# Rows of the experts' results leave through ScalarE's DMA queue instead of GpSimd's

## The chip, the cores and the metric
One core of a Trainium2 chip. The time is the device time of one execution in microseconds, the median over runs. A core has TensorE (PE), VectorE (DVE), ScalarE (ACT), GpSimd (POOL) and SyncE (SP), and 16 DMA engines that serve the queues of all of them. SP's and ScalarE's transfers go through hardware queues, GpSimd's through a software queue.

## The reference
A decoder trunk of two layers over 1024 tokens of width 1024, in float32. Each layer is: a mixer (attention in layer 0; a state-space layer and gated DeltaNet in layer 1), a mixture of 32 experts of which each token takes two, and a gated embedding:

```
h = h + mixer(rms_norm(h))
h = h + hier_moe(rms_norm(h))      # per expert: (silu(x @ w_gate) * (x @ w_up)) @ w_down, 1024 -> 512 -> 1024
h = h + sigmoid(rms_norm(h) @ w_g + b_g) * (p @ w_p)
```

The change touches the experts' stage alone. Its weights are 32 x 3 matrices of 2 MB in a layer, about 201 MB.

## The kernel before, in words
**The experts' block.** Before it, GpSimd scatters each token's row to a region of its expert in DRAM (`slots_in`). `first_blocks` (from L1615) then works through units of 128 rows. A unit is a whole expert (the first two), or parts of two experts: 64 + 64 or 96 + 32 rows. There are 21 units in a layer (`units`, from `expert_units`, L1065). `weight_order` (L1094) fixes in which order the 2 MB tiles of w_gate, w_up and w_down are loaded, and into which of eight places of a ring each goes. SP issues these loads (L1669), each after the product that used the place's last tile.

**The engines in one unit n.** TensorE: the first half of the gate product of unit n, the transposes of the hidden rows of unit n-1 (L1736), the second half of the gate product, the two halves of the down product of n-1, the transposes of the rows of n+1 (`turn`, L1716), the up product of n. All products stand on L1724. ScalarE: Silu of the gate (L1788), a copy of the first half of the results of unit n-1 (`y_half`, L1781), a copy of the transposed rows of n+1 (`turned_out`, L1775). VectorE: a copy of the transposed hidden rows (L1801), the second half of the results (L1807), gate times up (L1840). GpSimd: `rows_in(n + 2)` brings the rows of unit n+2 from `slots_in` once the rows of unit n are transposed (L1689), and `rows_out(n - 1)` takes the results of unit n-1, once ScalarE and VectorE have both copied their half, to `slots_out` in DRAM (L1695). A part of a unit is one transfer. The expert's number is known when the kernel is built for the first two; for the others it is loaded from a table on the chip into a register of the issuing engine.

**What orders the work around it.** There are two buffers for the rows and two for the results, taken by even and odd units. `y_half` on both engines waits for the results of two units earlier to have left (`y_out`). The last unit's results don't go through `rows_out`: SP issues them (`last_rows`, L1679). SP does this after the embedding's own loads (L1948 to L1958), which are in the same block of the program and wait for places of the ring to come free. Then SP waits for all results to be in DRAM and gives `all_out` (L1564). The embedding's part (`layer_embedding`, from L1962) has GpSimd gather two rows of `slots_out` for each token (L2010), VectorE add them to h (L2172, L2175), and the gate product follow on TensorE (L2080).

**Overflow.** `overflow_blocks` handles rows beyond an expert's share; with these inputs its loop runs over nothing.

Of the kernel before, what the change touches and what calls it, by code (L numbers as in the profile page):

```python
# [15 lines left out]
P = 128  # L16
# [1032 lines left out]
EXPERTS = GROUPS * PER_GROUP  # L1049
REGION = S + P // 2  # L1050
ROUTES = GROUPS + EXPERTS
HEAVY, FIXED, FIRST = 18, 2, 1e5
# [12 lines left out]
def expert_units():  # L1065

    heavies, lights = list(range(FIXED, HEAVY)), list(range(HEAVY, EXPERTS))
    ranks, units = list(range(FIXED)), [[Part(q, 0, P)] for q in range(FIXED)]  # L1070
    trios, pairs = len(heavies) // 2, (len(lights) - len(heavies) // 2) // 2
    assert 2 * trios == len(heavies) and trios + 2 * pairs == len(lights)

    def pair():
        q = len(ranks)
        ranks.extend([lights.pop(0), lights.pop(0)])
        units.append([Part(q, 0, 2 * QUAD), Part(q + 1, 2 * QUAD, 2 * QUAD)])

    for n in range(pairs - 1):
        pair()  # L1080
    for n in range(trios):
        q = len(ranks)
        ranks += [heavies.pop(0), heavies.pop(0), lights.pop(0)]
        units += [[Part(q, 0, 3 * QUAD), Part(q + 2, 3 * QUAD, QUAD)],
                  [Part(q + 1, 0, 3 * QUAD), Part(q + 2, 3 * QUAD, QUAD, QUAD)]]
    pair()
    return ranks, units
# [527 lines left out]
def first_blocks(nc, c, t, layer, r, ch, ring, preloaded, place, joint):  # L1615
# [6 lines left out]
    views = expert_weights(t, layer)  # L1622
    KF = FF // P
    _, units = expert_units()
    UNITS = len(units)
    tiles, places, last_user = weight_order(units)
    at_tile = {tile: n for n, tile in enumerate(tiles)}
    arrivals = [sum(len(units[m]) for m in range(n % 2, n + 1, 2)) for n in range(UNITS)]
    with scope(joint) as ctx:
        xb, y = place[:, 0:2], place[:, 2:4]  # L1630
# [8 lines left out]
        with stage(nc, *[f"tile{n}_in" for n in range(RING)], "x_turned", "x_copied", "gated", "silued", "upped", "hidden", "h_turned",  # L1639
# [3 lines left out]
            x_in, y_out = c.x_in, c.y_out  # L1643
# [14 lines left out]
            @block.sync  # L1658
            def _(sp):
                expert = {}  # L1660
                for n in range(preloaded, len(tiles)):
                    kind, q = tiles[n]
                    if q not in expert:
                        expert[q] = q if q < FIXED else sp.value_load(r.table[0:1, 3, q:q + 1], min_val=0, max_val=EXPERTS - 1)
                    before = [x for x in range(n) if places[x] == places[n]]
                    if before:
                        used, by = tiles[before[-1]][0], last_user[tiles[before[-1]]]
                        sp.wait_ge((gated, upped, downed)[used], (2 if used == 2 else 1) * (by + 1))
                    sp.dma_start(ring[places[n]].rearrange("p (k n) -> p k n", k=KF if kind == 2 else KD),  # L1669
                                 views[kind][expert[q]]).then_inc(tile_in[places[n]], 16)  # L1670
                clear_used(sp)
                last_expert.update(expert)
# [8 lines left out]
            @block.gpsimd  # L1681
            def _(pool):
                expert = {q: q for q in range(FIXED)}

                def rows_in(n):
                    for x in units[n]:
                        if x.q not in expert:
                            expert[x.q] = pool.value_load(r.table[0:1, 3, x.q:x.q + 1], min_val=0, max_val=EXPERTS - 1)
                        pool.dma_start(xb[x.row:x.row + x.rows, n % 2], c.slots_in[bass.ds(expert[x.q] * REGION + x.slot, x.rows), :]).then_inc(x_in[n % 2], 16)  # L1689

                def rows_out(n):
                    pool.wait_ge(y_act, n + 1)
                    pool.wait_ge(y_dve, n + 1)
                    for x in units[n]:
                        pool.dma_start(c.slots_out[bass.ds(expert[x.q] * P + x.slot, x.rows), :], y[x.row:x.row + x.rows, n % 2]).then_inc(y_out[n % 2], 16)  # L1695

                for n in range(UNITS):
                    if n + 2 < UNITS:
                        pool.wait_ge(x_turned, n + 1)
                        rows_in(n + 2)  # L1700
                    if n:
                        rows_out(n - 1)
                for n in (UNITS - 3, UNITS - 2):
                    pool.wait_ge(y_out[n % 2], y_before[n % 2] + 16 * arrivals[n])

# [63 lines left out]
            @block.scalar  # L1769
            def _(act):  # L1770
                def turned_out(n):
                    act.wait_ge(x_turned, n + 1)
                    if n >= 2:
                        act.wait_ge(upped, n - 1)
                    act.activation(xbt[:, n % 2].rearrange("p k t -> p (k t)"), turned[:], ACT.Copy).then_inc(x_copied, 1)  # L1775

                def y_half(n):
                    act.wait_ge(downed, 2 * n + 1)
                    if n >= 2:
                        act.wait_ge(y_out[n % 2], y_before[n % 2] + 16 * arrivals[n - 2])  # L1780
                    act.activation(y[:, n % 2, 0:SLAB], py[:, 0:SLAB], ACT.Copy).then_inc(y_act, 1)  # L1781

                turned_out(0)
                for n in range(UNITS):
                    act.wait_ge(gated, n + 1)
                    if n:
                        act.wait_ge(hidden, n)
                    act.activation(gate, pg[:], ACT.Silu).then_inc(silued, 1)  # L1788
                    if n:
                        y_half(n - 1)  # L1790
                    if n + 1 < UNITS:
                        turned_out(n + 1)
                y_half(UNITS - 1)

            @block.vector
# [1629 lines left out]
```

## Time and profile before

| | us |
|---|---|
| median of 3 runs | 3043.67 |
| lowest, highest | 3043.55, 3053.84 |
| the profiled execution's own time | 3048.08 |
| its span | 3046.6 |
| TensorE busy, ScalarE busy, GpSimd busy | 2795.1, 662.1, 249.7 |

The span is from the first to the last instruction in the trace; the execution's own time is taken around it. The experts' stages lie at about 830 to 1400 us and 2340 to 2920 us. "Busy" does not count the issuing of a transfer by SP or ScalarE; rows of such issues carry the name of the queue (SPq, ACTq). GpSimd's issues are counted as busy.

### The profile page before, as it was taken

What the parts mean: (1) busy time and instruction counts of PE and PEld (TensorE: products, weight loads), DVE (VectorE), ACT (ScalarE), POOL (GpSimd) and SP (SyncE); (2) the same over time, 40 slices, a digit from 0 to 9 for tenths busy, and PEclk for the clock granted to TensorE, in tenths of its full rate; (3) what the DMA queues carried; (4) which work ended last, traced back from release to release, by engine and by line L of the source; (5) the groups of instructions that cost most, each with busy time, mean ns of one, the idle gap of its engine ahead of it and who ended that gap; (6) DMA issues with size and microseconds to landing.
All of it is one profiled execution on the core that took longest, in us unless ns stands there. A gap on an engine that the chain in (4) does not pass through costs nothing. (4 is left out here: it accounts for less than half of the span.)

```text
span 3046.6 us, 40782 instructions
## 1 busy us (share of the span) xinstructions
PE 2795.1 (92%) x16517; PEld 1438.2 (47%) x16518; DVE 1113.5 (37%) x2450; ACT 662.1 (22%) x1262; POOL 249.7 (8%) x376
## 2 busy tenths in 40 slices
PE   7999999999898898989989999877998989888998
PEld 4644555555642232324467744477655323222343
DVE  2585455544400000004464725566464000000053
ACT  3310355541110000003421124422211000000132
POOL 0000000000100000002000000044211000000020
PEclk9999999999899999999999999998998999999999
DMA  4000693012599999996020120000417999999931
GB/s 162 28 20 8 243 408 123 1 65 99 218 353 397 397 397 397 401 410 218 35 67 1 16 71 28 0 2 2 175 63 271 368 399 397 399 400 393 400 127 42
DMA packets 137045, 609.37 MB, mean 200 GB/s; under 512 B 25700, under 2 KB 32260, under 8 KB 120456
## 3 DMA queue, kind: packets, MB, share of 16 engines
q1 hardware_dynamic: 111848, 529.08, 44.7%
q0 software_dynamic: 21632, 74.46, 6.9%
q10 hardware_dynamic: 3376, 3.19, 0.3%
q8 instruction: 133, 2.18, 0.3%
q14 instruction: 56, 0.46, 0.0%
HBM read 503.80 MB, written 101.71 MB: 199 GB/s over the span
## 5 line engine op out<-in xcount | busy, mean ns | idle before, releaser
L2775 PE MATMUL acc<-xt,work 128*128 128x512 f32 x384 | 166.9, 593 | 0.0
L672 PE MATMUL acc<-h,xt 128*128 128x512 f32 x384 | 165.2, 592 | 0.0
L310 PE MATMUL scores<-xt 65*128 65x512 f32 (+7 forms) x384 | 146.0, 489 | 0.4 <-DVE xt L451 0.4
L1724 PE MATMUL pg<-place 128*32 128x512 f32 (+2 forms) x736 | 137.8, 594 | 2.5 <-issue 2.5
L457 DVE TENSOR_REDUCE nmax<-scores 128x1 f32<-128x256 f32 (+7 forms) x128 | 96.8, 756 | 74.0 <-PE scores L312 70.4
L672 PEld LDWEIGHTS acc<-h,xt 128*128 128x128 f32 x384 | 72.9, 190 | 91.1 <-issue 90.9
L1724 PE MATMUL pu<-place 128*32 128x512 f32 (+2 forms) x768 | 115.1, 639 | 0.5 <-issue 0.5
L1221 PE MATMUL acc<-place 128*128 128x512 f32 x256 | 112.7, 594 | 1.1 <-PEq L71 1.1
L2775 PEld LDWEIGHTS acc<-xt,work 128*128 128x128 f32 x384 | 72.0, 190 | 86.1 <-issue 86.1
L1807 DVE COPY place<-py 128x512 f32<-128x512 f32 x21 | 14.5, 692 | 230.0 <-PE py L1724 230.0
L1807 DVE COPY work<-py 128x512 f32<-128x512 f32 x21 | 14.5, 691 | 228.9 <-PE py L1724 228.9
L404 ACT ACTIVATE s_t<-scores,nmax 128x256 f32<-128x256 f32 (+7 forms) x128 | 94.3, 736 | 8.0 <-DVE nmax L457 6.6
L1724 PE MATMUL py<-place 128*32 128x512 f32 (+2 forms) x608 | 86.5, 606 | 9.1 <-issue 7.9
L768 ACT ACTIVATE place<-acc 128x256 f32<-128x256 f32 (+4 forms) x88 | 39.8, 473 | 243.1 <-PE acc L672 243.0
L1840 DVE TENSOR_TENSOR work<-work,pu 128x512 f32<-128x512 f32 x21 | 14.4, 688 | 201.6 <-PE pu L1724 201.6
L1840 DVE TENSOR_TENSOR place<-place,pu 128x512 f32<-128x512 f32 x21 | 14.4, 688 | 200.0 <-PE pu L1724 200.0
L2449 PE MATMUL acc<-s_t,xt 128*128 128x260 f32 (+1 forms) x256 | 85.5, 496 | 1.1 <-PEq L71 1.1
L310 PEld LDWEIGHTS scores<-xt 65*128 65x128 f32 (+1 forms) x384 | 62.8, 190 | 33.1 <-issue 32.7
L1788 ACT ACTIVATE place<-pg 128x512 f32<-128x512 f32 x21 | 12.5, 597 | 293.4 <-PE pg L1724 293.4
L1724 PE MATMUL pg<-xt,place 128*32 128x512 f32 (+2 forms) x400 | 75.0, 601 | 1.3 <-ACT place L1775 1.1
L672 PE MATMUL acc<-place,xt 128*128 128x392 f32 (+1 forms) x256 | 76.1, 453 | 0.0
L1724 PE MATMUL pg<-own,work 128*32 128x512 f32 (+2 forms) x400 | 74.8, 601 | 1.4 <-ACT work L1775 1.1
(761 smaller groups left out, 5435.5 us busy)
## 6 DMA issues: line engine op xcount, KB each, us to landing
place<-in_moe_w_gate_dram SPq DMA_DIRECT2D x21, 2048.0 KB, 24.2
place<-in_moe_w_up_dram SPq DMA_DIRECT2D x20, 2048.0 KB, 26.3
slots_out<-zeros SPq DMA_DIRECT2D x4, 9216.0 KB, 63.0
place<-in_moe_w_down_dram SPq DMA_DIRECT2D x18, 2048.0 KB, 27.1
xt<-in_moe_w_up_dram SPq DMA_DIRECT2D x17, 2048.0 KB, 26.4
xt<-in_moe_w_gate_dram SPq DMA_DIRECT2D x16, 2048.0 KB, 23.6
xt<-in_moe_w_down_dram SPq DMA_DIRECT2D x15, 2048.0 KB, 29.1
s_t<-in_moe_w_up_dram SPq DMA_DIRECT2D x11, 2048.0 KB, 26.8
```

The costliest lines, as they stand in the source:

```text
L310: pe.matmul(bank(n, u)[:, a * SLAB:a * SLAB + w], qkt[0:kind(p).rows, p % 2, u, 0, i * P:(i + 1) * P], qkt[0:kind(p).rows, p % 2, u, 1, a ...
L404: act.activation(probs[:, u, n % 2, 0:(i + 1) * P], bank(n, u), ACT.Exp, bias=nmax[:, n % 2, u:u + 1], accum_out=total[:, (n // NT) % 2, i ...
L457: dve.tensor_reduce(nmax[:, n % 2, u:u + 1], bank(n, u), AX.X, ALU.max, negate=True).then_inc(maxed, 1)
L672: last = pe.matmul(acc[:, n % 4, 0:width], xs[:, k, tile_of(i)], weights[:, k, cols], start=(k == 0), stop=(k == k_of - 1))
L768: last = act.activation(place, part, ACT.Copy)
L1221: last = pe.matmul(acc[:, n, :], columns(k, i), slabs[n][:, k, :], start=(k == 0), stop=(k == KD - 1))
L1724: last = pe.matmul(out[part], lhs[:, k, part], weights_of(kind, q)[:, k, cols], start=(k == 0), stop=(k == k_last), skip_group_check=True)
L1788: act.activation(gate, pg[:], ACT.Silu).then_inc(silued, 1)
L1807: dve.tensor_copy(y[:, n % 2, SLAB:D], py[:, SLAB:D]).then_inc(y_dve, 1)
L1840: dve.tensor_tensor(hid, gate, pu[:], ALU.mult).then_inc(hidden, 1)
L2449: ins = pe.matmul(acc[:, n % 4, 0:width], xt[:, k, at], slab[:, k, 0:width], start=(k == 0), stop=(k == KD - 1))
L2775: last = pe.matmul(acc[:, n % 4, :], slabs[m // 4 % 2][:, k, (m % 4) * P:(m % 4 + 1) * P], xt[:, k, half * SLAB:(half + 1) * SLAB], start= ...
```

## The change
`rows_out` moves from GpSimd's program to ScalarE's. GpSimd keeps `rows_in` alone. ScalarE issues the transfers of unit n-1 after the copy of the transposed rows of unit n+1, waits for both halves of the results first, and loads the experts' numbers into its own registers. The last unit's results stay with SP.

```diff
-                def rows_out(n):
-                    pool.wait_ge(y_act, n + 1)
-                    pool.wait_ge(y_dve, n + 1)
-                    for x in units[n]:
-                        pool.dma_start(c.slots_out[bass.ds(expert[x.q] * P + x.slot, x.rows), :], y[x.row:x.row + x.rows, n % 2]).then_inc(y_out[n % 2], 16)
-
-                for n in range(UNITS):
-                    if n + 2 < UNITS:
-                        pool.wait_ge(x_turned, n + 1)
-                        rows_in(n + 2)
-                    if n:
-                        rows_out(n - 1)
+                for n in range(UNITS - 2):
+                    pool.wait_ge(x_turned, n + 1)
+                    rows_in(n + 2)
                 for n in (UNITS - 3, UNITS - 2):
                     pool.wait_ge(y_out[n % 2], y_before[n % 2] + 16 * arrivals[n])
...
+                expert = {q: q for q in range(FIXED)}
+
+                def rows_out(n):
+                    act.wait_ge(y_act, n + 1)
+                    act.wait_ge(y_dve, n + 1)
+                    for x in units[n]:
+                        if x.q not in expert:
+                            expert[x.q] = act.value_load(r.table[0:1, 3, x.q:x.q + 1], min_val=0, max_val=EXPERTS - 1)
+                        act.dma_start(c.slots_out[bass.ds(expert[x.q] * P + x.slot, x.rows), :], y[x.row:x.row + x.rows, n % 2]).then_inc(y_out[n % 2], 16)
+
                 turned_out(0)
                 for n in range(UNITS):
...
                     if n + 1 < UNITS:
                         turned_out(n + 1)
+                    if n:
+                        rows_out(n - 1)
                 y_half(UNITS - 1)
```

## Rows read from the trace of the kernel before

**Rows 1.** The page: busy us, share of the span and instructions of each engine.
```profile
PE 2795.1 (92%) x16517; PEld 1438.2 (47%) x16518; DVE 1113.5 (37%) x2450; ACT 662.1 (22%) x1262; POOL 249.7 (8%) x376
```

**Rows 2.** Windows: us, busy PE, PEld, DVE, ACT, POOL (instructions), TensorE clock, DMA share, GB/s.
```profile
820.00:1400.00 580.00, 524.36 (x3808) 187.09 (x3807) 55.81 (x111) 55.99 (x80) 47.92 (x86) 0.96 1.00 387
...
2440.00:2820.00 380.00, 335.79 (x2878) 110.88 (x2878) 29.68 (x43) 31.61 (x43) 29.12 (x58) 0.96 1.02 398
```

**Rows 3.** Waits of TensorE from 2440 to 2820 us: total, times, longest.
```profile
PE turned L1716 <- issue: 24.4, 8, 3.9
PE py L1724 <- issue: 13.4, 7, 3.4
PE py L1724 <- DMA own<-in_moe_w_down_dram: 2.7, 3, 1.3
```

**Rows 4.** Chain of waits (start, us) and SP's issues, 2560 to 2610 us.
```profile
2567.57 26.14 DMA own<-in_moe_w_down_dram
...
2600.83 2.77 issue
...
2568.05 8.60 SPq L1669 DMA_DIRECT2D xt<-in_moe_w_up_dram  x2
```

**Rows 5.** Chain of waits, end of the second layer's experts: start, us, what.
```profile
2865.76 5.26 SPq L1952
...
2871.07 7.64 SPq L1954
...
2885.74 10.97 DMA slots_out<-work
```

**Rows 6.** Groups of ScalarE, 820 to 1400 us: busy, mean ns, idle before, releaser.
```profile
L1788 ACT ACTIVATE place<-pg 128x512 f32<-128x512 f32 x21 | 12.5, 597 | 293.4 <-PE pg L1724 293.4
```

**Rows 7.** Instructions of L1695: ns min/median/max; last its time to landing.
```profile
L1695 POOL DMA_DIRECT2D slots_out<-work x38: 489/510/583, 2373.5 to 2867.8; - x38
DMA to landing us min/median/max: 5.7/7.0/10.8
```

**Rows 8.** Timeline of GpSimd, 2470 to 2476 us; landing of its rows in (L1689).
```profile
2472.32 1.13 POOL L1695 DMA_DIRECT2D slots_out<-work  x2 [22.92 <-DVE work L1807]
2474.17 0.51 POOL L1689 DMA_DIRECT2D work<-slots_in  x1 [0.72 <-issue]
2475.37 0.49 POOL L1689 DMA_DIRECT2D work<-slots_in  x1 [0.69 <-issue]
...
DMA to landing us min/median/max: 7.6/9.0/17.3
```

**Rows 9.** SP's issues of the last rows: instructions of L1679, and the timeline.
```profile
L1679 SPq DMA_DIRECT2D slots_out<-place x2: 479/537/595, 1379.2 to 1380.0; - x2
...
2884.95 1.29 SPq L1679 DMA_DIRECT2D slots_out<-work  x2
```

**Rows 10.** Timeline of VectorE, 2860 to 2900 us.
```profile
2865.77 0.69 DVE L1807 COPY work<-py 128x512 f32<-128x512 f32 x1 [9.93 <-PE py L1724]
```

**Rows 11.** Timeline of ScalarE: one unit, and the last copy of y.
```profile
2499.36 1.02 ACT L1775 ACTIVATE work<-turned 128x1024 f32<-128x1024 f32 x1 [7.87 <-PE turned L1716]
2515.59 0.60 ACT L1788 ACTIVATE work<-pg 128x512 f32<-128x512 f32 x1 [15.20 <-PE pg L1724]
...
2879.67 0.60 ACT L1781 ACTIVATE work<-py 128x512 f32<-128x512 f32 x1 [16.74 <-PE py L1724]
```

**Rows 12.** DMA queues, 2440 to 2820 us: packets, MB, share of 16 engines.
```profile
q1 hardware_dynamic: 17513, 135.93, 89.6%
q0 software_dynamic: 4507, 14.79, 11.6%
```

**Rows 13.** DMA queues, 2867 to 2876 us.
```profile
q0 software_dynamic: 160, 0.52, 14.5%
```

**Rows 14.** SP's issues of weights (L1669), the group with the longest: ns min/median/max.
```profile
L1669 SPq DMA_DIRECT2D xt<-in_moe_w_up_dram x16: 332/453/6542, 844.8 to 2789.7; - x16
```

**Rows 15.** Timeline of VectorE, end of the first layer's experts.
```profile
1378.23 0.69 DVE L1807 COPY place<-py 128x512 f32<-128x512 f32 x1 [10.76 <-PE py L1724]
```

## Prediction

> **What bounds the kernel now.** The page first [rows 1]: TensorE is busy for 92% of the span and ScalarE for 22%, so a change of who issues a transfer can only matter where TensorE stops. The windows by stage say where that is [rows 2]: between 2440 and 2820 us, in the second layer's experts, TensorE is busy for 335.79 of 380 us, and the DMA column stands at 1.02 of the 16 DMA engines' time. Those engines have no free time there. The waits of TensorE in that stretch [rows 3] name a w_down tile for 2.7 us and "issue" for 37.8 us (24.4 + 13.4). I read most of that "issue" as weights too. In the chain of one pair of units [rows 4] the down products end at 2600.83 and TensorE starts on the turn of the next unit 2.77 us later. What stands between them in the code is the wait for the w_up tile. SP issued two w_up tiles in a run from 2568.05 to 2576.65, and I give them 26 to 27 us to land (26.14 is what the w_down tile before them took). The second one then lands near 2603, an estimate from these rows. So the loop is: a product ends and frees a tile place, SP issues the next 2 MB, and it lands 25 to 27 us later because others are under way: 2.1 MB at 398 GB/s is 5.3 us, so about five share the DMA engines. The bound is bytes over the DMA rate, with TensorE a close second, and the first layer is the same again.
>
> At the end of the block another chain takes over [rows 5]: SP issues the last unit's rows behind its issues of the embedding's weights, and the second transfer lands 10.97 us after 2885.74, at 2896.71; GpSimd's gathers wait for that.
>
> **The change, part by part.** The moved transfers are those of all units but the last. There are 21 units in a layer [rows 6], and the group on L1695 counts 38 transfers a layer, 76 in all [rows 7].
>
> 1. GpSimd loses 38 issues a layer, at 510 ns in the median [rows 7]. Its issues of rows for unit n+2 come up to 1.2 us earlier (two issues back to back took 1.13 us, at 2472.32 [rows 8]). These rows are wanted by TensorE's turn of unit n+2, more than one whole unit later (21 units in 580 us: 27 us each [rows 2]) and land in 9 us in the median [rows 8]. So they are not late now, and an earlier issue is worth 0.
>
> 2. ScalarE gains, in each unit, two waits, two issues and up to two loads of an expert number. SP issues the very same form of transfer for the last unit: 479 to 595 ns for the issue itself, 1.29 us for a pair with the register work between them [rows 9]. A load of the expert number is not shown on ScalarE. The nearest rows are GpSimd's: without loads a pair takes 1.13 us, so about 0.56 each; with a load between, the next issue starts 1.20 us after the one before (2474.17 to 2475.37) [rows 8]. That is about 0.65 us a load. Together 1.3 + 2 x 0.65 = 2.6 us a unit. Below, the bound is 0.5 us (issues overlapped with what ScalarE runs); above, I add two holds by SP (below). 28 loads a layer come in place of GpSimd's.
>
> They stand right after the turned copy (L1775). The y_act they wait for is ScalarE's own, done one operation earlier. The y_dve comes 0.69 us after the second down product [rows 10]; the turned copy, which itself takes 1.02 us [rows 11], can only begin after eight transposes that follow that product, so this wait costs nothing. Queued behind are the Silu of the next unit, which waits 293.4 us over 21 for TensorE's gate product, 14.0 us each [rows 6]. In the timeline: copy at 2499.36, done at 2500.38, next Silu at 2515.59, so 15 us of room [rows 11]. 2.6 of 14 us: price 0.
>
> 3. The DMA engines' work. The bytes are the same, and so is the number of row packets. What may differ is what a byte costs on the software and on the hardware queue. Over 2440 to 2820 us [rows 12] the hardware queue moved 135.93 MB in 89.6% of 380 x 16 engine-us, 24.95 GB/s an engine; the software queue 14.79 MB in 11.6%, 20.97 GB/s. But that queue carries rows in and rows out mixed. Between 2867 and 2876 us only rows out were on it [rows 13]: 0.52 MB in 14.5% of 9 x 16 = 144 engine-us, 25 GB/s. So the expensive ones are the rows in, which stay where they are. Rows out already cost what the weights cost. I take 0. The two bounds: with 20 units of 0.524 MB, 10.49 MB a layer, the mixed rate gives 500 engine-us against 420 on the hardware queue, 80/16 = 5 us saved a layer, 10 us in all; the other way, if such a write cost a tenth more on ScalarE's queue, 2.6 us a layer lost, 5 in all.
>
> 4. SP. While ScalarE issues, SP may have to wait. In the loop this delays a weight transfer's start by some 0.5 us while about five others are under way, and DMA stands at 1.02: nothing. At the end of the block it does not stand under that cover. The rows of the last unit but one are ready at 2866.46 (DVE's copy from 2865.77, 0.69 us [rows 10]), and SP issues nearly without a break from 2865.76 until it takes up the last rows at 2884.95 [rows 5, 9]. Two issues of 0.54 us in between would move SP's last rows by up to 1.1 us in this layer. But SP's issues are long there (7.64 us at L1954) against 0.33 us for a 2 MB tile where it is not held (the shortest of L1669 [rows 14]), so they wait for room in the queue, and that room comes at the same time whoever else issues. In layer 0 the last rows are issued at 1379.2 [rows 9], right after DVE's copy, which ends at 1378.92 [rows 15]; the copy is what they wait for, and a delay of SP is hidden there in part. I take 0.5 us for both layers together, with 0 and 2.2 as ends.
>
> The sum is 0 + 0 + 0 + 0.5. On the profiled execution's own time, 3048.08 us (the span 3046.6 and 1.5 around it), that is 3048.6. The profiled execution is 4.4 us above the median of the runs shown (3043.67), so in those terms 3044.2; I say 3044.
>
> A rule weighed against this. The trace shows SP in one issue for as long as 6542 ns in the loop [rows 14], and 7.64 us at the end [rows 5]; ScalarE issues no transfer in those stretches, so no row shows what it would do then. The Trainium skill (Perfetto Trace Analysis, DMA Instruction — HWDGE) states that the hardware descriptor generator is shared by the sequencers that use it and locked for one at a time, with the lock wait inside the profiled time. By that rule ScalarE would stand behind SP in such a stretch; by the rows alone it would not. Where it changes the time, it is the second rival.
>
> **Rivals.**
> Rows out get cheaper on the hardware queue. For it: the software queue's share per MB, 19% above the other one's in the mixed window. Against it: the window with rows out alone. Worked out above: 10 us less, 3034. If something else of the software path goes with it, such as GpSimd's issues of rows being late for TensorE, it would be more: the waits "issue" at TensorE's turn, 24.4 us in 380, are the only room, and if half of them were really rows in that come late, both layers would give 24 us, 3020. Against that: these rows land in 9 us and have 20. The Trainium skill (SBUF — State Buffer, the "DVE blocks DMA" trap) has software descriptors starved while VectorE copies; here GpSimd issues rows out only after VectorE's copy has ended and takes 489 to 583 ns each time, so no row shows a starved one.
>
> Slower, by one mechanism: the hardware queues of SP and ScalarE exclude each other while one issues. Place one is ScalarE, held in rows_out. It decides once it is held for more than about 11 us after the turned copy (14.0 less 2.6), because the Silu is then late and with it TensorE's next up product and gate. One hold in the loop is at most 6.5 us, so that needs two in a row. Place two is the block's end: if SP always goes first, ScalarE gets free only near 2884.9 instead of issuing at 2866.5, its last copy of y, at 2879.67 now [rows 11], comes 5 to 6 us late, and SP's last rows, which wait for it, go out near 2886.7 (two issues, 1.3, and the copy, 0.6, later): 1.8 us; in both layers about 3: 3047. Place three is SP, held by 76 issues of 0.54 us. If none of that were covered, 41 us, 3085; but for this the DMA engines would have to run dry, and nothing in rows 2 says so. A middle case, with ten or so late Silus or tiles of 2 us, is 3064.
>
> The change does not do what it says. Rows out landed in 7.0 us (5.7 to 10.8) before [rows 7]. Nobody waits for them inside the loop, because y of unit n is written again two units later. So a faster or slower landing changes nothing either way, and the time stays at 3044.
>
> **How the numbers follow.** Forecast, with the last rival, which gives the same time: 0.78. Cheaper rows by up to 10 us: 0.07. GpSimd's rows were late, 3020 or so: 0.04. Exclusion with a small price at the ends (3047): 0.06; with late Silus or tiles (3064 and up): 0.05. What a measurement of this kernel tells from no change is 0.5%, 15.2 us. Faster by more: 0.04, and 0.01 for what I don't see, 0.05. Slower by more: 0.05 and 0.02 for the same, 0.07. Within: 0.88. Range 3032 to 3058: the low end is the full 10 us and a little of the runs' own spread (3043.55 to 3053.84), the high end that spread with the price at the block's ends.
>
> **What would show it.** The page after: GpSimd's issues on the old line gone and 76 issues on ScalarE's queue; the small hardware queue q10 up by some 21 MB and the software queue down by as much. TensorE busy as before, DMA at 1.0 from 2440 to 2820, and the mean of GB/s within 1% of 398. ScalarE's issues near 0.54 us where SP is not in an issue; several us where it is, if the two exclude each other. The Silu still ended by TensorE's gate product. The chain at the end through SP's issues and the last rows as before. Wrong would be: a Silu released by anything but TensorE, TensorE idle for weights while the DMA share is under 1, or a stretch of the experts that is shorter by 5 us or more a layer.

## The result, and the profile after

The changed kernel takes 3022.18 us (median of 4 runs, 3019.68 to 3028.07), the kernel before 3044.39 beside it (4 runs). The ratio is 0.9917, with a 95% interval of 0.99 to 0.9933: 22 to 25 us less, where no change was forecast. A second measurement, the run change_again, gave 0.9916 (0.9899 to 0.9932).

The page of the changed kernel answers to [rows 1] like this:

```profile
PE 2797.8 (92%) x16517; PEld 1445.1 (48%) x16518; DVE 1114.0 (37%) x2450; ACT 662.6 (22%) x1262; POOL 210.9 (7%) x300
```

Only GpSimd has less to do than before. What has changed stands in the windows, which answer to the second row of [rows 2]:

```profile
2440.00:2820.00 380.00, 350.19 (x3024) 114.90 (x3020) 30.38 (x44) 32.22 (x44) 13.73 (x28) 0.96 1.02 411
```

The DMA engines are as full as before (1.02), but they move 411 GB/s, not 398, and TensorE gets through 3024 products in the window instead of 2878. The queues from 2440 to 2780 us (packets, MB, share of 16 engines), first before, then after:

```profile
q1 hardware_dynamic: 15969, 121.22, 89.3%
q0 software_dynamic: 4160, 13.63, 11.9%
```
```profile
q1 hardware_dynamic: 16357, 124.53, 89.7%
q0 software_dynamic: 2180, 7.17, 5.8%
q10 hardware_dynamic: 2225, 7.32, 5.7%
```

Read as MB over engine time (share x 340 x 16 us): before, the weights on q1 went at 24.95 GB/s an engine and the rows on q0 at 21.1. After, the weights go at 25.5, the rows in on q0 at 22.7 and the rows out on q10 at 23.6. So the gain is not mainly on the moved transfers. The weights, which nobody touched, have become cheaper.

A short window shows where. From 2499.4 to 2509.4 us before, and from 2492.5 to 2499.5 us after, the rows out and the rows in of one unit both move (1.04 MB of rows in each window):

```profile
DMA packets 912, 3.63 MB, mean 363 GB/s; under 512 B 89, under 2 KB 89, under 8 KB 891
```
```profile
DMA packets 723, 2.66 MB, mean 380 GB/s; under 512 B 77, under 2 KB 77, under 8 KB 722
```

Against 420 GB/s (the mean of the stage in the run wide_in below), 10 us at 363 lose 1.4 us and 7 us at 380 lose 0.7. That is 0.7 us a unit, and with 38 such units some 26 us, an estimate from these two windows.

ScalarE's new issues, the instructions of its line (ns min/median/max), and how long they took to land:

```profile
L1782 ACTq DMA_DIRECT2D slots_out<-work x38: 321/322/537, 2366.3 to 2847.7; - x38
...
DMA to landing us min/median/max: 6.0/7.7/11.8
```

They are shorter than the 0.54 us that I took, and none is held: the longest, in the first layer, has 563 ns. At 2847.19 ScalarE issues a pair in 0.81 us in the middle of SP's issue of 4.77 us (L1955, at 2845.74 in the chain below):

```profile
2847.19 0.81 ACTq L1782 DMA_DIRECT2D slots_out<-work  x2
```

The timelines of ScalarE and GpSimd in one unit of the changed kernel show where they stand:

```profile
2464.27 1.43 ACTq L1782 DMA_DIRECT2D slots_out<-work  x2
```
```profile
2464.71 0.51 POOL L1689 DMA_DIRECT2D work<-slots_in  x1 [23.60 <-issue]
2465.86 0.49 POOL L1689 DMA_DIRECT2D work<-slots_in  x1 [0.64 <-issue]
```

Rows out and rows in are now issued within half a microsecond of each other, on two queues. Before, they stood in one queue, out first, in 1.9 us later [rows 8], or 4.7 to 5.2 us later in the units between (2495.78 and 2501.01 in the next one). So the change did two things: it gave the rows out a queue of their own, and, as ScalarE issues them behind its turned copy, it moved them next to the rows in.

Where in the kernel: GpSimd's first gather after the experts starts at 1375.28 instead of 1389.97 in the first layer, and 1.5 us of these 14.7 were there before the block (the first copy of transposed rows starts at 832.45, not 833.95). That leaves 13.2 us. In the second layer the last scatter before the block starts at 2320.12 instead of 2326.35, the first gather at 2876.88 instead of 2897.08: 14.0 us. The sum is 27, or 28.6 with the 1.5; the spans differ by 20.2 (3046.6 and 3026.4). The rest is lost in between. From the first gather to the last scatter before the second block, which is mostly the second layer's mixer, it takes 936.4 us before and 944.8 after. The granted clock of TensorE differs there. From 1600 to 1800 us, before, after, and in the run called mirror below:

```profile
1600.00:1800.00 200.00, 190.68 (x919) 134.07 (x918) 100.51 (x252) 34.84 (x59) 7.34 (x21) 0.98 0.14 33
```
```profile
1600.00:1800.00 200.00, 191.29 (x887) 131.42 (x887) 93.25 (x188) 34.49 (x57) 7.35 (x21) 0.94 0.14 33
```
```profile
1600.00:1800.00 200.00, 190.95 (x909) 128.50 (x909) 95.59 (x203) 35.11 (x58) 7.35 (x21) 1.00 0.14 33
```

The clock there is 0.94 after and 1.00 in mirror, whose profiled execution took 3021.44 us against 3028.07. The same stage takes 943.0 us in change_again, a second profile of the changed kernel, 933.2 in mirror, 943.1 in apart and in two_wide, and 935.6 in over_read. Two_wide has its rows out on GpSimd and over_read on ScalarE, so the stage's length does not go by the engine that issues them. What sets it stays open; it puts up to 12 us into the times below that do not come from the experts' stages.

The chain at the end of the second layer's block is the same as in [rows 5], 20 us earlier: SP's issues of the embedding's weights, the last rows landing in 10.37 us, the gathers.

```profile
2845.74 4.77 SPq L1955
...
2850.55 8.68 SPq L1957
...
2859.27 4.64 SPq L1959
...
2863.96 1.11 SPq L1961
...
2866.14 10.37 DMA slots_out<-work
```

### The profile page after: what moved, and what is told of

It is laid out like the page before. It is cut to its first block and busy times, and to the rows that moved or that the text cites. A ratio compares the mean times of both kernels' runs of the same rounds, so it can differ in the third digit from the quotient of the medians.

```text
span 3026.4 us, 40948 instructions
## 1 busy us (share of the span) xinstructions
PE 2797.8 (92%) x16517; PEld 1445.1 (48%) x16518; DVE 1114.0 (37%) x2450; ACT 662.6 (22%) x1262; POOL 210.9 (7%) x300
## 5 line engine op out<-in xcount | busy, mean ns | idle before, releaser
L1789 ACT ACTIVATE work<-pg 128x512 f32<-128x512 f32 x21 | 12.5, 597 | 296.4 <-PE pg L1715 296.4
## 6 DMA issues: line engine op xcount, KB each, us to landing
xt<-in_moe_w_up_dram SPq DMA_DIRECT2D x17, 2048.0 KB, 25.5
```

## The experiments

"Ratio" is to the kernel before on the same chip, with the 95% interval. In all of them the DMA share from 2440 to 2780 us is 1.02 (1.01 where said), so the column of GB/s says directly what the engines got done in full time. "Stages" is the time of the two experts' stages together, in the one profile of each run: from the last scatter before a block to the first gather after it, so without what lies between the blocks.

| run | what is different | median us | ratio | stages, us | GB/s, 2440 to 2780 |
|---|---|---|---|---|---|
| before | | 3044 to 3050 | 1 | 1140 | 398 |
| changed kernel | rows out on ScalarE | 3022.18, 3023.37 | 0.9917, 0.9916 | 1111, 1116 | 410 |
| mirror | rows in on ScalarE | 3021.92 | 0.9899 (0.9847 to 0.9952) | 1118 | 409 |
| apart | the change, rows out one Silu later | 3051.61 | 0.9995 (0.9973 to 1.0017) | 1142 | 399 |
| both_act | both on ScalarE | 3046.94 | 0.9989 (0.9966 to 1.0012) | 1142 | 397 |
| alternate | both on GpSimd, part by part in turn | 3046.55 | 0.9973 (0.9952 to 0.9994) | 1137 | 400 |
| landed | the change, rows in after rows out have landed | 3070.55 | 1.0069 (1.0049 to 1.009) | 1165 | 388 |
| thin_out | before, rows out cut to 64 bytes | 2998.68 | 0.9838 (0.982 to 0.9857) | 1093 | 397 |
| wide_in | before, rows in over 128 partitions | 2998.61 | 0.9839 (0.9821 to 0.9858) | 1092 | 420 (1.01) |
| wide_change | the same on the changed kernel | 3006.81 | 0.9857 (0.9829 to 0.9886) | 1093 | 421 (1.01) |
| two_wide | wide_in as two transfers | 3005.75 | 0.9855 (0.9835 to 0.9876) | 1094 | 420 (1.01) |
| quarters | before, rows in over 32 partitions | 3064.38 | 1.0059 (1.0037 to 1.0081) | 1151 | 392 |
| over_read | see below | 3029.76 | 0.9943 (0.9925 to 0.9961) | 1124 | 411 (1.01) |

### Queue or overlap: apart, both_act, mirror, alternate

Two theories stood first. A: what helps is that the two bursts of rows move beside each other. B: the software queue is the dearer one.

**apart** puts the same issue on the same queue, 14 to 19 us after the rows in (below, against the changed kernel):

```diff
                     act.activation(gate, pg[:], ACT.Silu).then_inc(silued, 1)
+                    if n >= 2:
+                        rows_out(n - 2)
                     if n:
                         y_half(n - 1)
                     if n + 1 < UNITS:
                         turned_out(n + 1)
-                    if n:
+                    else:
                         rows_out(n - 1)
```

> The change, but ScalarE issues the rows out one Silu later, some 14 us after the rows in of the same turn, so on their own queue but no longer beside rows in. Theory A (overlap: the two bursts now run beside each other, so the DMA engines spend fewer us in the slow regime that a burst of rows in makes): the gain is lost, ratio to before 0.998 to 1.002, 3038 to 3050 us. Theory B (the software queue itself is the dearer one for rows out): the gain stays, ratio 0.990 to 0.994, 3014 to 3026 us.

Measured 0.9995: the gain is gone, with rows out still on ScalarE's queue. In one unit the rows in and the rows out are issued at:

```profile
2482.22 0.49 POOL L1689 DMA_DIRECT2D work<-slots_in  x1 [0.65 <-issue]
```
```profile
2500.27 1.80 ACTq L1782 DMA_DIRECT2D slots_out<-work  x2
```

Its trace also separates the two kinds of rows, which the trace of before mixes. From 2440 to 2780 us:

```profile
q1 hardware_dynamic: 15720, 121.90, 89.5%
q0 software_dynamic: 1987, 6.57, 6.7%
q10 hardware_dynamic: 2080, 6.82, 5.0%
```

Rows out alone cost 25.1 GB/s an engine (6.82 MB in 5.0% of 5440 engine-us), rows in alone 18.0. And here is the same kernel during one burst of rows in (2462.2 to 2465.8 us) and during one of rows out (2447 to 2453 us), DMA's total first:

```profile
DMA packets 317, 1.10 MB, mean 306 GB/s; under 512 B 48, under 2 KB 48, under 8 KB 317
...
q1 hardware_dynamic: 222, 0.84, 75.4%
q0 software_dynamic: 95, 0.26, 27.5%
```
```profile
DMA packets 268, 2.57 MB, mean 429 GB/s; under 512 B 48, under 2 KB 48, under 8 KB 132
...
q1 hardware_dynamic: 152, 2.23, 86.8%
q10 hardware_dynamic: 116, 0.34, 14.2%
```

While rows in are on the way everything is slow, the weights included: 306 GB/s. While rows out are, nothing is: 429. (The weights' packets differ too, all under 8 KB in the first, half of all packets larger in the second; wide_in below shows that 4 KB packets are not what slows them.)

**both_act** moves `rows_in` into ScalarE's program as well, behind `rows_out`:

```diff
                 turned_out(0)
+                rows_in(2)
...
                     if n:
                         rows_out(n - 1)
+                    if n + 3 < UNITS:
+                        rows_in(n + 3)
```

> Rows out and rows in both go through ScalarE's hardware queue, out first and in behind it, none through GpSimd. Theory A (overlap of two queues): rows in stand behind rows out again, one after the other, so no gain: ratio 0.998 to 1.003. Theory B (software queue dearer per packet): double the gain of the change, since rows in leave it too: ratio 0.980 to 0.988.

0.9989: no gain without any software queue in the loop. Theory B is out.

**mirror** is the exchange: `rows_in` in ScalarE's program at the place that `rows_out` has in the changed kernel, `rows_out` alone in GpSimd's.

```diff
-                for n in range(UNITS):
-                    if n + 2 < UNITS:
-                        pool.wait_ge(x_turned, n + 1)
-                        rows_in(n + 2)
-                    if n:
-                        rows_out(n - 1)
+                for n in range(UNITS - 1):
+                    rows_out(n)
```

> Rows in through ScalarE's queue, rows out stay with GpSimd: the mirror image of the change, issued at nearly the same moment. Theory A (overlap): the same gain as the change, ratio 0.989 to 0.994. Theory B (software queue dearer for rows out): no gain, 0.998 to 1.002; if it is dearer for rows in, a gain by the queue alone, then to be told apart by both_act.

0.9899: the whole gain, with rows out still on GpSimd. What counts is that there are two queues and nearly one moment: in mirror the two are issued 0.3 us apart in one unit (2457.04 and 2457.29) and 2.8 us apart in the next (2481.03 and 2483.84).

**alternate** keeps GpSimd's one queue and issues a part out, a part in, in turn:

```diff
+                    for at in range(max(len(outs), len(ins))):
+                        if at < len(outs):
+                            rows_out(n - 2, outs[at:at + 1])
+                        if at < len(ins):
+                            rows_in(n + 2, ins[at:at + 1])
```

> All on GpSimd's queue as before, but the parts alternate: a part out, a part in, a part out, a part in. Theory A in its wide form (any mixing of the two directions helps): part of the gain, ratio 0.993 to 0.998. Theory A in its narrow form (it takes two queues, within one queue the packets go in order): 0.998 to 1.002. Theory B (queue kind): 0.998 to 1.002.

0.9973 (0.9952 to 0.9994): at most a small part. It doesn't decide between the two forms that I had written down.

### The overlap again: landed

```diff
                 for n in range(UNITS - 2):
                     pool.wait_ge(x_turned, n + 1)
+                    if n >= 2:
+                        pool.wait_ge(y_out[n % 2], y_before[n % 2] + 16 * arrivals[n - 2])
                     rows_in(n + 2)
```

> The change as it is on ScalarE, but GpSimd waits until the rows out of the same turn have landed before it issues rows in (7 to 9 us later; TensorE wants them more than 20 us later). Theory A (the gain is that rows out and rows in move beside each other): the gain goes, ratio to before 0.998 to 1.002. Rival (apart lost the gain for its late place on ScalarE, behind the next Silu): the gain stays, 0.990 to 0.994.

The gain went, as theory A had it, but the kernel became slower than before by 0.7%, which neither theory had. Two bursts of rows in of this kernel, 2452.6 to 2461 and 2482.5 to 2490.5 us:

```profile
DMA packets 292, 2.77 MB, mean 330 GB/s; under 512 B 47, under 2 KB 47, under 8 KB 148
...
q0 software_dynamic: 132, 0.41, 15.9%
```
```profile
DMA packets 281, 2.64 MB, mean 330 GB/s; under 512 B 48, under 2 KB 48, under 8 KB 144
```

144 packets of the 292 are larger than 8 KB here, against none of 317 in apart's burst: later by 8 us, rows in meet the loads of w_gate and w_up instead of w_down's. 0.41 MB of rows take 8.4 us (on q0, in the first of the two stretches), where apart moved 0.26 MB in 3.6 us, and the whole goes at 330 GB/s for all that time. I read it as rows that wait behind larger packets; the trace gives packets and times, not the order in which an engine takes them, so this is not shown. It matters not only that rows in have company, but which.

### Is it the rows out: thin_out

```diff
-pool.dma_start(c.slots_out[bass.ds(expert[x.q] * P + x.slot, x.rows), :], y[x.row:x.row + x.rows, n % 2])
+pool.dma_start(c.slots_out[bass.ds(expert[x.q] * P + x.slot, x.rows), 0:16], y[x.row:x.row + x.rows, n % 2, 0:16])
```

> The kernel before, rows out cut to 64 bytes a row (the results that the tokens get are wrong), so the DMA engines have about 10.3 MB less a layer. At 400 GB/s that is 26 us a layer and 52 in all if the bytes bound, ratio 0.983; TensorE may take part of it. Theory A: the rows in are still alone with the weights and slow, so the mean rate from 2450 to 2780 us stays at or under 398 GB/s. Rival (rows out as such slow the others down, in whichever queue): the rate goes up to 405 or more and the ratio under 0.980.

0.9838 where the bytes alone gave 0.983, and the rate stays at 397. The weights, from 2440 to 2780 us:

```profile
q1 hardware_dynamic: 16140, 127.54, 94.1%
```

That is 24.9 GB/s an engine, as before (24.95), with almost nothing going out. Rows out cost their bytes and slow nobody down. The rows in do that, most of all where they move without company.

### Why rows in are slow: wide_in, wide_change, two_wide, quarters

The tiles of weights go to 128 partitions, the rows in of a unit to 96 and 32, or to 64 and 64. Theory C takes the difference from there, theory D from the reading side.

```diff
-                    for x in units[n]:
-                        pool.dma_start(xb[x.row:x.row + x.rows, n % 2], c.slots_in[bass.ds(expert[x.q] * REGION + x.slot, x.rows), :]).then_inc(x_in[n % 2], 16)
+                    x = units[n][0]
+                    pool.dma_start(xb[:, n % 2], c.slots_in[bass.ds(expert[x.q] * REGION, P), :]).then_inc(x_in[n % 2], 16)
```

> The kernel before, but the rows in of a unit are one transfer over all 128 partitions from the first expert's region (the second expert of a unit gets wrong rows); same bytes, same queue, still behind rows out. Theory C (rows in are slow because a transfer over 96, 64 or 32 partitions gives its 16 engines shares that lie on the SBUF ports of other engines' weights, while one over 128 partitions gives each engine its own port): the slow stretch goes, ratio 0.988 to 0.994 with no overlap at all. Theory D (reading the rows from DRAM is what is slow): 0.998 to 1.002.

0.9839: 49 us less, twice what the change gives, with the same bytes, in GpSimd's one queue, behind the rows out. That is more than C had been given (0.988 to 0.994). D as I had put it, that any reading of the rows from DRAM is slow, is out. The queues from 2440 to 2780 us, and one stretch with a burst, 2447.8 to 2453.8 us:

```profile
q1 hardware_dynamic: 16798, 128.38, 90.6%
q0 software_dynamic: 4112, 14.16, 10.3%
```
```profile
DMA packets 638, 2.52 MB, mean 420 GB/s; under 512 B 59, under 2 KB 59, under 8 KB 626
...
q1 hardware_dynamic: 418, 1.81, 74.5%
q0 software_dynamic: 220, 0.70, 29.2%
```

The weights go at 26.05 GB/s an engine now, the rows, out and in together, at 25.3, and a burst runs at 420 GB/s although 626 of 638 packets are small. The slow stretch is gone.

**wide_change** is the same edit on the changed kernel.

> The same 128-partition rows in, on the changed kernel (rows out by ScalarE). Theory C: nothing is left for the overlap to win, so within 0.3% of wide_in; ratio 0.985 to 0.993. Theory D: as the changed kernel, ratio 0.990 to 0.994, with wide_in at 1.00.

0.9857 against 0.9839, with intervals that overlap, and the two stages take 1093 us against 1092; the 8 us between the medians do not come from there. The stretch between the two blocks takes 944.9 us in this profile and 933.6 in wide_in's. With wide rows in, the overlap wins nothing. What the change wins is about half of that same loss, and nothing beside it. Here the rows in are alone on q0, from 2440 to 2780 us, and go at 25.6 GB/s an engine:

```profile
q0 software_dynamic: 1872, 6.82, 4.9%
```

**two_wide** answers the objection that wide_in also halves the number of transfers:

```diff
+                        for half in range(2):
+                            cols = slice(half * SLAB, (half + 1) * SLAB)
+                            pool.dma_start(xb[:, n % 2, cols], c.slots_in[bass.ds(expert[x.q] * REGION, P), cols]).then_inc(x_in[n % 2], 16)
```

> As wide_in (rows in from the first expert's region alone, on the kernel before), but in two transfers over all 128 partitions, each with half the columns: the number of transfers is again that of before, and the packets are 2 KB. Theory C (the partitions that a transfer spans decide): the gain stays for the larger part, ratio 0.982 to 0.990. Rival E (wide_in won by halving the number of transfers, or by one transfer in place of two): 0.997 to 1.002.

0.9855, 420 GB/s. Its packets did not become 2 KB, as I had expected: the software queue has 4160 packets with 13.63 MB, as before, so the run changes the number of transfers alone. **quarters** goes the other way, with each row from its own expert: four transfers over 32 partitions in each unit.

```diff
+                        for at in range(0, x.rows, QUAD):
+                            pool.dma_start(xb[x.row + at:x.row + at + QUAD, n % 2], c.slots_in[bass.ds(expert[x.q] * REGION + x.slot + at, QUAD), :]).then_inc(x_in[n % 2], 16)
```

> The kernel before with rows in as four transfers over 32 partitions each in every unit (right rows). Theory C: no transfer spans 128 partitions, as before, so the slow stretch stays or grows: ratio 0.999 to 1.006. Rival E (what counts is how many bytes or transfers stand behind each other): a clear change in either way by the number of transfers, 1.01 or more.

1.0059, at the upper end of what C was given, 392 GB/s. The number of transfers does not order these runs: one and two wide ones are fast, two and four narrow ones slow. The span of partitions does. One difference is left in it: each wide transfer also reads its 128 rows from one expert's region of DRAM, and no run reads those same rows over a narrow span. Against a reason on that side stands quarters, which reads the same rows as the kernel before, only split further over the partitions, and is slower; and over_read below, where a transfer of 32 rows out of one region is slow and one of 128 is not.

The Trainium skill has a mechanism that would fit. SBUF — State Buffer (Door 1: The DMA port swizzle) states that partitions are reached through 16 ports, and that partitions 0 to 63 reach no more of them than 0 to 31. The Trainium skill, DMA: Bandwidth & Descriptors (The descriptor swizzle), states that in a transfer over 128 partitions each of the 16 engines writes one port of its own. The runs agree as far as they go: narrow spans slow the weights down with them, 128 partitions don't. That it is the ports on which the shares of a narrow transfer meet those of the weights is an inference; no trace here shows a port, and what the Trainium skill says of partitions 0 to 63 does not cover the transfers over 96 partitions.

### A version that computes the reference: over_read

wide_in, wide_change and two_wide compute from wrong rows for the second expert of a unit. A version that doesn't has the first transfer span 128 partitions, and puts the other expert's 32 rows over it when it has landed:

```diff
+                    shared = units[n][0].rows == 3 * QUAD
+                    for at, x in enumerate(units[n]):
...
+                        if shared and at:
+                            pool.wait_ge(x_in[n % 2], x_before[n % 2] + 16 * (arrivals[n] - arrivals[n % 2]) - 16)
+                        rows = P if shared and not at else x.rows
```

> A version with right results on the changed kernel: in the 16 units of 96 + 32 rows the first transfer of rows in spans all 128 partitions (32 rows too many), and the second, after the first has landed, puts the 32 right rows over them. Theory C: only a quarter of the rows comes through a narrow transfer; 0.31 us a unit for the bytes too many against up to 0.6 us of slow regime saved: 0 to 10 us under the changed kernel, ratio to before 0.988 to 0.993. If C is wrong: the extra bytes alone, 10 us slower than the changed kernel, 0.994 to 0.997.

> The changed kernel itself, beside over_read on the same chip: ratio to before 0.990 to 0.994, as measured.

3029.76 against 3023.37 for the changed kernel on the same chip: slower by 6 us. By what I had written beforehand this speaks against theory C: its 0.9943 lies outside C's range (0.988 to 0.993) and inside the one that I had given if C were wrong (0.994 to 0.997). The trace says what C had left out. First one wide transfer beside rows out (2545.6 to 2549.9 us), then the small one of the same unit (2555.1 to 2557.1 us):

```profile
DMA packets 494, 1.80 MB, mean 419 GB/s; under 512 B 54, under 2 KB 54, under 8 KB 494
```
```profile
DMA packets 115, 0.72 MB, mean 358 GB/s; under 512 B 18, under 2 KB 18, under 8 KB 89
```

The wide transfer is no longer slow: 419 GB/s. The changed kernel has 363 while its rows in move beside rows out (2494.4 to 2499.3 us):

```profile
DMA packets 508, 1.78 MB, mean 363 GB/s; under 512 B 74, under 2 KB 74, under 8 KB 508
```

But the small one goes alone with the weights, some 9 us later, and is slow as in landed. And 0.13 MB more go in with each of 16 units a layer, which at 411 GB/s is 10 us in both layers, an estimate. The stage's rate of 411 GB/s, hardly above the changed kernel's 410, has these bytes in it. So the run fits C once the small transfer has its price, but that was added afterwards. Of the kernels that compute the reference, the changed one and its mirror stay the fastest. A gather of all 128 rows by index was not tried.

## Why the prediction was wrong

**The step that failed is the third, the DMA engines' work.** It had the right question, and even the number that answers it: the software queue's MB cost 19% more than the weights' [rows 12], and rows out alone did not [rows 13]. The conclusion was that the dear ones are the rows in, "which stay where they are", so 0, with 10 us as the upper bound. Measured: 22 us in the medians, 27 in the two blocks. Two things in it are wrong, as the runs showed.

- The price of a transfer was taken to be its own. It depends on what moves beside it: rows in go at 18.0 GB/s an engine alone with the weights (apart), 22.7 beside rows out (after), 25.6 over 128 partitions (wide_change).
- The comparison was made with 24.95 GB/s for the weights as if that were their proper rate. It held the loss already. With rows in over 128 partitions they go at 26.05 (wide_in). In 4858 engine-us of 5440, that is the larger part: 121.22 MB at 26.05 are 4653 engine-us, 205 less, or 12.8 us of every 340.

In all, 49 us of the kernel before go with the narrow rows in (wide_in). Why company with the rows out takes back about half of that is not shown: the runs show that the rate while rows in move is 306 GB/s alone (apart) and 363 beside rows out (after), not what happens in an engine.

**The first rival** had the right sign, for a reason that fell: "cheaper on the hardware queue" is refuted by both_act and apart. Its larger form, rows in that come late for TensorE, fell with apart as well: there GpSimd has rows in alone and issues them as early as in the changed kernel, and nothing is won. That its figure, 3020, lies close to the measured 3022 is luck.

**What held.** The bound (bytes over the DMA rate, DMA share 1.02 before and after), though the rate itself, which was to stay within 1% of 398, rose to 411. The sign of being wrong that was named, a stretch of the experts shorter by 5 us or more a layer, came: 13 and 14 us. Step 1, GpSimd's time worth nothing. Step 2: ScalarE took two issues with their loads in 0.8 to 1.8 us, below my 2.6, and the Silu still waited for TensorE alone (285.5 us over 21 in the first layer, 13.6 each, against 14.0 in [rows 6]). Step 4: no delay of SP; the end of the block runs as before. The second rival, exclusion of the two hardware queues, didn't show: ScalarE's longest issue has 563 ns, and it issued a pair at 1344.15 in 0.81 us while SP was in one of 11.05 us (from 1342.77).

**What I should have done.** The bound was a rate, so each change of what is in flight at the same time had to be priced as a change of that rate. The trace of before had it. From 2501 to 2505 us, with rows out moving, and from 2506.5 to 2510.5 us, with rows in, it shows:

```profile
DMA packets 425, 1.65 MB, mean 413 GB/s; under 512 B 37, under 2 KB 37, under 8 KB 420
```
```profile
DMA packets 369, 1.32 MB, mean 330 GB/s; under 512 B 47, under 2 KB 47, under 8 KB 369
```

Four to five microseconds a unit at 330 instead of 413 GB/s are about 0.9 us, and there are 38 such units in the two layers: some 35 us, as an estimate from these two lines.

## What to carry to other kernels

Where the DMA engines are the bound, look at the rate in short windows, not over the stage: a dip of the total while a small transfer is under way is that transfer's true price, and the big one pays it. Let small loads that span fewer than 128 partitions run beside stores, not alone with the bulk loads; better, give them 128 partitions. Which engine issues is worth little in itself, but two queues let two things meet that one queue keeps apart, and moving one of them away takes the gain back: by 9 us in landed, by 14 to 19 us in apart. Nearly 3 us, in every second unit of mirror, did not.

## What the runs showed of the hardware that I had not expected

- A load over 96 + 32 partitions slowed down all that was in flight with it, to 306 to 330 GB/s; over 128 partitions the same bytes ran at 420 (wide_in). A store over the same partitions did not: 429 (apart).
- Which of the two bursts had the hardware queue and which the software one made no difference (mirror 409, the changed kernel 410 GB/s), and with both in one queue there was no gain, hardware (both_act, 397) or software (before, 398).
- ScalarE issued a row transfer in 322 ns in the median, SP the same form in 537, the median of two [rows 9]. SP's long issues did not hold ScalarE: 0.81 us for a pair inside one of 4.77 us.
